# Down products of gathered experts in three fp32r passes, with GpSimd making the weights' low parts, and adaLN pieces two per step in the experts on all tokens

## The reference

```python
g_sel = argmax(g_logits)                       # one group of experts for each token
top_v, top_i = top_k(e_logits of that group, 2)
for n in range(32):
    a, b = split(h @ w_up[n], 2)               # 1024 -> 2 x 256
    out += combine[:, n:n+1] * ((silu(a) * b) @ w_down[n])   # 256 -> 1024
```

## Time and profile before

| what | value |
|---|---|
| median of 3 runs | 1899.25 us (1898.12 to 1901.4) |
| the profiled execution, device time | 1907.31 us |
| its span, first to last instruction | 1905.5 us |
| mean granted TensorE clock | 0.992 |
| PE busy | 1853.0 us, 97% |
| DVE, ACT, POOL busy | 1166.6, 775.0, 0.2 us |
| HBM traffic | 389.66 MB, mean 204 GB/s |
| the mixture's steps 2 to 39 with what ends them | about 369 to 735 us of the span |

### The profile page before, as it was taken

How to read it: one execution, slowest core, us unless ns; L and a number is a source line. 1 busy time by engine, 2 the same in 40 slices (tenths; PEclk the granted TensorE clock), 3 DMA queues, 4 the chain that set the end, 5 groups by cost and what they waited for, 6 DMA issues and landing times.

```text
span 1905.5 us, 29853 instructions
## 1 busy us (share of the span) xinstructions
PE 1853.0 (97%) x12440; PEld 1666.4 (87%) x12440; DVE 1166.6 (61%) x1774; ACT 775.0 (41%) x1078; POOL 0.2 (0%) x4
## 2 busy tenths in 40 slices
PE   9999989899999999999999999999999999989999
PEld 8889879688866667999988889999999997879999
DVE  3594445666666646877647448776876547545443
ACT  2324533444444445343443234444444444325432
POOL 0000000000000000000000000000000000000000
PEclk9999999899999999999999999999999999999999
DMA  7334310566799976777440057876676341033451
GB/s 311 132 133 155 133 66 1 221 241 255 300 391 364 390 317 257 307 305 283 194 139 23 23 199 262 325 307 267 266 301 260 156 155 45 8 148 121 191 199 67
DMA packets 65222, 391.59 MB, mean 206 GB/s; under 512 B 7360, under 2 KB 7488, under 8 KB 27328
## 3 DMA queue, kind: packets, MB, share of 16 engines
q1 hardware_dynamic: 64800, 389.61, 53.0%
q10 hardware_dynamic: 288, 0.08, 0.0%
HBM read 388.61 MB, written 1.05 MB: 204 GB/s over the span
## 4 chain that ended last, share of the span: by engine, by line
PE 89%; DVE 6%; ACT 3%; DMA 1%; issue 1%; SPq 0%; DVEq 0%; ACTq 0%
PE bank L510 87%; PE bank L551 1%; DMA slab<-in_w_up 1%; ACT w_hi L1442 1%; DMA slab<-in_w_ffn_in 1%; DVE slab_low L1886 0%; DVE region L1950 0%; DVE tiny L1931 0%; DVE region L2479 0%; DVE region L2456 0%; DVE region L2477 0%; DVE hT L1871 0%; ACT rsB L1365 0%; DVE region L1930 0%; DVE slab_low L1967 0%
## 5 line engine op out<-in xcount | busy, mean ns | idle before, releaser
L1886 DVE TENSOR_TENSOR slab_low<-slab,w_hi 128x2048 fp32r<-128x2048 f32 x152 | 348.1, 2291 | 207.0 <-ACT w_hi L1442 206.8
L510 PE MATMUL bank<-h_hi,w_hi 128*128 128x256 f32 x1408 | 394.9, 280 | 1.5 <-DVE h_lo L1878 1.5
L510 PE MATMUL bank<-h_lo,w_hi 128*128 128x256 f32 x1408 | 396.0, 281 | 0.0
L510 PE MATMUL bank<-h_hi,slab_low 128*128 128x256 f32 x1408 | 394.9, 280 | 0.0
L1442 ACT ACTIVATE w_hi<-slab 128x2048 fp32r<-128x2048 f32 x152 | 291.1, 1916 | 163.3 <-DMA slab<-in_w_up 80.7
L510 PEld LDWEIGHTS bank<-h_hi,slab_low 128*128 128x128 f32 x1408 | 268.8, 191 | 0.0
L510 PEld LDWEIGHTS bank<-h_hi,w_hi 128*128 128x128 f32 x1408 | 264.7, 188 | 3.0 <-issue 3.0
L510 PEld LDWEIGHTS bank<-h_lo,w_hi 128*128 128x128 f32 x1408 | 264.6, 188 | 0.0
L510 PE MATMUL bank<-gT_hi,d_hi 128*128 128x256 f32 x832 | 233.8, 281 | 0.8 <-DVE gT_lo L2083 0.8
L510 PE MATMUL bank<-gT_lo,d_hi 128*128 128x256 f32 x832 | 233.7, 281 | 0.0
L510 PE MATMUL bank<-gT_hi,d_low 128*128 128x256 f32 x832 | 233.7, 281 | 0.0
(11 more groups left out here) (279 smaller groups left out, 2752.6 us busy)
## 6 DMA issues: line engine op xcount, KB each, us to landing
slab<-in_w_ffn_in SPq DMA_DIRECT2D x88, 1024.0 KB, 8.5
slab<-in_w_up SPq DMA_DIRECT2D x64, 1024.0 KB, 9.2
region<-in_w_ada SPq DMA_DIRECT2D x112, 512.0 KB, 6.6
region<-in_w_ffn_out SPq DMA_DIRECT2D x44, 1024.0 KB, 4.8
region<-in_w_down SPq DMA_DIRECT2D x32, 1024.0 KB, 5.7
slab<-in_w_in SPq DMA_DIRECT2D x23, 1024.0 KB, 4.8
slab<-in_w_mix_in SPq DMA_DIRECT2D x20, 1024.0 KB, 8.6
hT<-in_w_ada SPq DMA_DIRECT2D x32, 512.0 KB, 5.9
```

The costliest lines, as they stand in the source:

```text
L510: return nc.tensor.matmul(o, lhsT, rhs, start=start, stop=True, skip_group_check=True)
L1886: V_.tensor_tensor(slab_low[slot][:, :], slab[slot][:, :], w_hi[h % 3][:, :].bitcast(F), ALU.subtract)\
```

## The change

Few units now get the three passes too. `down_few` multiplies `gT_hi` by the high and low parts of the down weights and `gT_lo` by the high part: 12 fp32r matmuls of 512 columns instead of 4 float32 ones. ACT makes `d_hi` of few unit u at the end of step s of the same unit, after its second `up_high`; GpSimd makes `d_low`; DVE makes `gT_lo` in every step. The weights' high parts of few units alternate between two places, and the scatter's matrix moves from the region to `rsB` and to the place of the router's weights. `ada_slot` now gives the mixture's 32 pieces two per step, to steps 1 to 16; the two places and the waits of `ada_loads` stay as they are.

```diff
@@ def ada_slot(seg, r):
-    return [p for p in range(n) if 1 + p // rate == r]
+    return [p for p in range(n) if 1 + p // (rate if seg else 2) == r]
@@ def build
-        permT = zone(28 * KB, (N_GROUP - 1) * T).rearrange("p (i t) -> p i t", i=N_GROUP - 1)
+        permT = [rsB[:, 0:T], rsB[:, T:2 * T], part["router"][:, 0:T]]
@@ def d_hi_of(unit):
-            return 0 if unit.seg == 0 else unit.u % 2
+            return 0 if unit.kind == "full" else (unit.u + 1) % 2
@@ def bank_free(s, seg):
-                elif unit.split:
+                else:
                     pe.wait_ge(S["gt_lo"], low_steps(old))
-                else:
-                    pe.wait_ge(S["gt_hi"], old + 1)
@@ def down_few(unit, middle=None):
-                pe.wait_ge(S[f"d_in{b}"], 16 * (unit.u // 2 + 1))
-                pe.wait_ge(S["gt_hi"], unit.steps[-1] + 1)
+                pe.wait_ge(S["dlo_few"], unit.u - PER_GROUP + 1)
+                pe.wait_ge(S["gt_lo"], low_steps(unit.steps[-1]))
@@
-                        m = mm(bank[2 + half][:, :], gT_few[b][:, j, :], rows_[:, j, half * 512:(half + 1) * 512],
-                               unit.x == 0 and j == 0)
+                        o, cols = bank[2 + half][:, :], slice(half * 512, (half + 1) * 512)
+                        mm(o, gT_hi[b][:, j, 0:P], hi[:, j, cols], unit.x == 0 and j == 0)
+                        mm(o, gT_hi[b][:, j, 0:P], lo[:, j, cols])
+                        m = mm(o, gT_lo[b][:, j, 0:P], hi[:, j, cols])
@@ ScalarE: down_high(unit)
-                k = unit.u - (1 if unit.seg == 0 else 2)
+                k = unit.u - (1 if unit.kind == "full" else 2)
                 if k >= 0:
                     act.wait_ge(S["down_done"], k + 1)
@@ ScalarE: moe(), the step's order
                     if unit is not None and s == unit.steps[-1]:
                         up_high(unit.halves[1] + 2)
+                    if unit is not None and unit.kind == "few":
+                        down_high(unit)
@@ VectorE: turned_low(s)
-                    if not unit.split:
-                        return
@@ GpSimd
+            for unit in UNITS:
+                if unit.kind == "few":
+                    b = unit.u % 2
+                    pool.wait_ge(S["dhi_ready"], unit.u + 1)
+                    nc.gpsimd.tensor_tensor(d_low[b][:, :], d_raw[b], d_hi[d_hi_of(unit)][:, :].bitcast(F),
+                                            ALU.subtract).then_inc(S["dlo_few"], 1)
```

More of the change, by code:

```diff
@@ L133 @@
     "ulo_ready": "the low part of half of a unit's up weights", "dlo_ready": "that of its down weights",
+    "dlo_few": "that of a gathered expert's down weights, by GpSimd",
     "gt_lo": "a step's turned activations, low part", "hg_low": "a chunk of the gathered h, low part",
@@ L183 @@
     halves: list
-    @property
-    def split(self):
-        return self.kind != "few"
 def plan():
@@ L464, in low_steps, with low_by_dve @@
         def low_steps(s):
-            return sum(len([x for x in u.steps if x <= s]) for u in UNITS if u.split)
-        def split_units(u):
-            return sum(1 for x in UNITS[:u + 1] if x.split)
+            return s + 1
+        def low_by_dve(u):
+            return sum(1 for x in UNITS[:u + 1] if x.kind != "few")
         def unit_of(s):
@@ L792, in down_split @@
                 b = unit.u % 2
-                pe.wait_ge(S["dlo_ready"], split_units(unit.u))
+                pe.wait_ge(S["dlo_ready"], low_by_dve(unit.u))
                 pe.wait_ge(S["gt_lo"], low_steps(unit.steps[-1]))
@@ L837, in down @@
             def down(unit, middle=None):
-                if unit.split:
+                if unit.kind != "few":
                     down_split(unit, unit.steps[0] == SLOTS_OF[unit.seg][0][2], middle,
@@ L1491, in turned_high @@
                     src = place(s)[:, 0:T].rearrange("p (a b) -> p a b", a=2)
-                    dst = gT_hi[b][:, :, t * P:(t + 1) * P] if unit.split else gT_few[b][:, :, :]
+                    dst = gT_hi[b][:, :, t * P:(t + 1) * P]
                     nc.scalar.activation(dst, src, ACT.Copy).then_inc(S["gt_hi"], 1)
@@ L1512, in moe @@
                         up_high(unit.halves[0] + 2)
-                        if unit is not members[0] and UNITS[unit.u - 1].split:
+                        if unit is not members[0] and UNITS[unit.u - 1].kind == "full":
                             down_high(UNITS[unit.u - 1])
@@ L1701, in _ @@
             up_high(1)
-            evac(permT[:, 0:2, :].rearrange("p i t -> p (i t)"), 512)
-            evac(permT[:, 2, :])
+            evac(rsB[:, :], 512)
+            evac(permT[2])
             moe()
@@ L1891, in down_low @@
                 b = unit.u % 2
-                dve.wait_ge(S["dhi_ready"], split_units(unit.u))
+                dve.wait_ge(S["dhi_ready"], unit.u + 1)
                 V_.tensor_tensor(d_low[b][:, :], d_raw[b], d_hi[d_hi_of(unit)][:, :].bitcast(F), ALU.subtract)\
@@ L2677, in _ @@
             w = Seen()
-            low_slabs = iter(low_used)
-            def split_slabs(n, w_hi):
-                for k in range(n):
-                    slot, _ = next(low_slabs)
-                    pool.wait_ge(S["phi_ready"], w("phi_ready"))
-                    nc.gpsimd.tensor_tensor(slab_low[slot][:, :], slab[slot][:, :], w_hi[k % 3][:, :].bitcast(F),
-                                            ALU.subtract).then_inc(S["plo_ready"], 1)
+            for unit in UNITS:
[4 more added lines that the diff above has]
+                                            ALU.subtract).then_inc(S["dlo_few"], 1)
 INPUTS = ["x", "mem", "w_in", "w_mem_kv", "w_br_a", "w_br_b", "w_br_m", "w_o", "w_up", "w_down", "c_2", "w_ada_2",
```

7 lines of the change are left out of this document (3 added, 4 removed).

## The result

The changed kernel takes 1985.43 us (median of 4 runs, 1984.41 to 1986.57), the kernel before in the same series 1900.33 us (4 runs, 1898.12 to 1905.39): a ratio of 1.0435, 95% interval [1.0414, 1.0457]. The direction was forecast, the size was not: 58 us forecast, 85.1 us measured on the medians. The profiled execution of the changed kernel has a span of 1982.6 us (device time 1984.41 us, mean granted clock 0.976), 77.1 us above the span of before. Of before's 7.0 us, 2.7 show in its trace ahead of the mixture, where the granted clock was 0.83 from 255 to 275 us and 1.00 in the changed kernel's; I could not place the rest.

A forecast was written before the change was run, and what follows sets the result against it. PE's path was taken as the bound, PE being busy 97% of the span. Load-order stalls 45.5, clock 5.7 and few units 7 us sum to 58 us, so 1899.25 + 58 = 1957 us; range 1930 to 1970 us.

The forecast's parts named there:

- part 2: adaLN pieces in full units: slabs wait behind the pair on SP, period 22.6 us against PE's 17.31; 45.5 us.
- part 3: Full units: lower PE clock after a stall slows the next 12 matmuls, 1.42 us for half of 8 stalls; 5.7 us.
- few units and group ends: Few units at 9.6 us each plus about half of the scatter's 3.44 us: 3 groups 3.6 us longer.
- end of the mixture: Last unit: nothing covers the low-part passes before its down product; with the chain's lag, 3.4 us.
- The first P: First delayed start by PE of a unit's second step: 388.2 instead of 379.58, 8.6 us later.
- landing 5.3 us: Full units' loop: an up slab lands 5.3 us after its load goes out on SP.
- Part 4: Few units' low parts: DVE and POOL passes take turns, POOL's 4.58 us, a unit 9.6 us; together +7 us.
- Rival A: Few units: DVE's and POOL's passes don't collide, 13 us come back, 1937.5 us; chance 0.36.
- Rival B: Full units: up loads no later where it counts, under 1.6 us a stall, 1886 us; chance 0.06.
- Rival C: Few units: POOL's pass takes 6.9 us, as three passes would, a unit 11.9 us, 2012 us; chance 0.04.
- Part 1: Few units' down product: 12 fp32r matmuls take 2.80 us instead of 3.41, 0.61 us off each of 24, 14.6 us.

The follow-up runs named there:

- e2: The kernel before with only the adaLN pieces moved, two per step in steps 1 to 16: 1983.66 us, ratio 1.0427.
- e3: The changed kernel with SP loading the pair for a unit's first step before the down weights, the second step's pair after: 1907.47 us, ratio 1.0015.
- e8: The changed kernel with the second piece of the pair ahead of the slabs sent behind them: 1977.03 us, ratio 1.039.
- e12: e8, with SP waiting until both places are free before it sends the first piece: 1970.53 us, ratio 1.0352.
- e6: The changed kernel with 14 unread matmuls behind the up product of each full unit's first step: 1969.79 us, ratio 1.0341.
- e1: The changed kernel with its adaLN pieces back to one per step, three-pass down products kept: 1932.3 us, ratio 1.0152.
- e5: e3, with DVE's `slab_low` of the few units reading one tensor instead of two, POOL kept: 1893.04 us, ratio 0.9948.
- e4: e3, with DVE instead of POOL making the few units' `d_low`, POOL idle: 1892.98 us, ratio 0.9943.
- e7: The changed kernel with a full unit's second slab, from the third unit on, sent only when the first has landed: 1984.91 us, ratio 1.0426.
- e11: The changed kernel with two extra 1 MB loads ahead of the pair in full units from the third on: 1987.15 us, ratio 1.0437.

## Why the prediction was right in direction and too small

By its own steps, on the span:

| step | forecast, us | measured, us |
|---|---|---|
| parts 2 and 3, turn 0 to 16 | 45.5 + 5.7 = 51.2 | 80.8 |
| few units and group ends, turn 16 to 39 | +3.6 | -2.4 |
| end of the mixture | +3.4 | +1.4 |
| sum | 58 | 79.8, and -2.7 ahead of the mixture |

- **The mechanism of part 2 was right.** The slab behind the pair on SP, with every link of the loop, stands in the chain, and one line of the change makes it all (e2); another order of the loads takes it away (e3). The first P came at 387.15, where before had 379.58; with the 2.7 us by which this execution was ahead, it is 10.3 us late for the 8.6 forecast.
- **The term "landing 5.3 us" was mis-sized.** It came from the one slab behind one piece. Behind two pieces it is 6.94, 7.83, 7.30, 6.76, 9.09, 8.00 and 6.94 us. The last six average 7.65: 2.35 us more in each period. The row was of another traffic pattern than the one after the change, and the trace of before already had slabs at 6.8 and 8.0 us; I took no upper bound for it. By e8 and e12 together the pattern is most of it: with one piece ahead and 0.6 us between the transfers the mean of seven is 5.8, without unit 8's. The rest stays open.
- **The term of part 3 was mis-sized too.** I let half of 8 stalls cost 1.42 us. Every one of them cost more: in seven the 12 matmuls took 4.58 to 5.49 us (mean 4.94) instead of 2.80, 2.14 us each, and the eighth, 60 matmuls in 11.03 us for the 8.47 of the earlier trace rows, cost 2.6, together 17.5 us. The row I used, with a granted clock of 0.79 over 8 us, followed a stall of 2 us; the new stalls are of 6.8 to 9.2 us and come in every unit. And the cost stands in the loop: PE's late turn delays the pair, so it adds to each period in full. 22.6 + 2.35 + 2.14 = 27.1 us, against 27.05 measured. Over the whole stretch the eight landings are 17.3 us above 5.3 each and the clock 11.8 above its 5.7: 29.1 of the 29.6 us by which 51.2 missed 80.8. e6 confirms the clock's size from the other side: 13.2 us come back when PE is kept busy.
- **Part 4 had the right mechanism**, turns between whole passes (e1, e5), and 4.58 us for POOL's pass was near: 4.48 in its turn, 4.64 undisturbed. The few unit came out at 9.17 us, not 9.6, because I added whole durations where the passes follow one another closer: `gT_lo` stands in the chain with 0.26 us and not 0.42, the `slab_low` behind POOL with 2.15 and not 2.29, and POOL with 4.48 and not 4.58. Against that the scatter's 3.4 us came in full and not by half. A group of eight takes 76.8 us for the 78.5 forecast. Before, the second group took 77.8 and not 77.3, since some of its units waited for late transfers. So few units end 2.4 us ahead of before and not 3.6 behind. The Trainium skill, "GPSIMD Engine Reference", section "Elementwise — side-by-side cycle accounting", has 4497 ns for POOL's pass; the trace shows 4.64 us beside a one-input DVE pass, 3% more.
- **Part 2's "the passes themselves move for nothing" was right for the full units and missed what they did in the few ones.** With POOL at work, a piece's pass in a few unit costs 1.8 us of a unit's time (11.0 for 9.17), by e1. The move was of use there. The 0.66 us of DMA time that part 2 saves in a few unit is wrong too: 0.52 MB at 400 GB/s are 1.3 us; no sum used it.
- **Rival A** (no collision) fell by the turns in the trace; its 8.62 us for a few unit is reached only without two-tensor passes on DVE beside POOL (e5), or without POOL (e4). **Rival B** (loads not late where it counts) needed a stall under 1.6 us; it was 9.7. **Rival C** (POOL's pass of 6.9 us) was wrong in its mechanism, though its time of 2012 us erred on the other side by about as much as mine, 27 us for 28. My range ended at 1970 us since it held A's case and 14 us for the clock, where my own bound of 2.80 us for each of 8 stalls gives 22, and no upper end for the landing: 9 us instead of 5.3 in seven periods is 26 us more, 1983 us. **Part 1** was right: 0.62 us a unit where nothing takes turns (e4).

## What to carry to other kernels

When a change makes a queue wait for something later, follow the loop once round (load, split, matmul, release, load): if its length is above what the engine needs, that length is the new period, and every slow link counts in full, here the landing under the new traffic and the low clock after a stall. Look for another order of the same loads before giving up the change: here it was worth 77 us. And before moving a pass to GpSimd, list VectorE's passes over two SBUF tensors beside it; each that fell beside it here waited for the whole GpSimd pass, and where VectorE had 2.3 us to spare the pass was better left there (e4).

## What the runs showed of the hardware that I had not expected

- A short pass suffers as much as a long one from POOL: 1.22 us became 5.59 (e1), 2.29 became 5.20, and `slab_low` on one input stayed at 2.29 with 2289 ns as its longest of 48 (e5). The short pass with one operand in a PSUM bank kept its 0.47 us beside POOL.
- A 1 MB load mostly lands in 5.3 us half a us behind one 512 KB load, and in 6.8 to 9.1 us behind two that are 1.15 us apart. What goes out behind it (e7) and whether the engines had work long before (e11) made no clear difference; closer spacing did (e12). The reading that the engines run dry between transfers and start slowly fits these runs, but isn't shown by itself, and it leaves unit 8's slab and single ones of 8 and 9 us unexplained.
- After a stall of 6.8 to 9.2 us PE ran its next 12 matmuls in 4.58 to 5.49 us where 2.80 is the time at 2.4 GHz, and twice that, 5.60, the time at 1.2 GHz; the granted clock at the start of one such stretch was 0.50. Matmuls whose result nobody reads, put into the stall (e6), gave 3.06 us, and 15.0 us less for the full units.
